# Wider small products and extra dense products on TensorE around the attentions and behind the experts of a four-layer transformer kernel

## What is computed

```python
o = jnp.stack(outs, axis=2) * alpha[..., None].astype(h.dtype)
return o.reshape(b, s, ATTN_WIDTH) @ w_o
...
for e in range(N_EXPERTS):
    out = out + gates[..., e:e + 1] * swiglu(h, w_gate[e], w_up[e], w_down[e])
```

## Time and profile before

| | |
|---|---|
| median of 3 runs | 2066.69 us (2065.45 to 2076.85) |
| the profiled execution's own time | 2066.5 us |
| its span, first to last instruction | 2064.3 us |
| mean granted TensorE clock over the span | 0.946 of full |
| TensorE busy | 1932.4 us (94%) |
| VectorE busy | 1639.3 us (79%) |
| ScalarE busy | 1138.9 us (55%) |
| DMA | 551.07 MB, mean 267 GB/s |

### The profile page before, as it was taken

How to read it: one execution, slowest core, us unless ns; L and a number is a source line. 1 busy time by engine, 2 the same in 40 slices (tenths; PEclk the granted TensorE clock), 3 DMA queues, 4 the chain that set the end, 5 groups by cost and what they waited for, 6 DMA issues and landing times.

```text
span 2064.3 us, 29232 instructions
## 1 busy us (share of the span) xinstructions
PE 1932.4 (94%) x9196; PEld 1602.1 (78%) x9196; DVE 1639.3 (79%) x2173; ACT 1138.9 (55%) x1616; POOL 36.1 (2%) x47
## 2 busy tenths in 40 slices
PE   2998999989899999999999999988899999789998
PEld 2987888867688888888888888866778888677886
DVE  6988886757898989998888989897686659677554
ACT  1434444443677777777777777654444444545443
POOL 2000000000000000000000000000000000000000
PEclk9999999977899999999999999987699999879999
DMA  8977996545699999999999999957368875735662
GB/s 290 340 248 268 346 360 199 148 157 176 201 358 335 366 340 368 330 366 335 344 355 340 361 337 363 339 173 218 111 223 265 270 243 145 255 123 175 218 217 73
DMA packets 368361, 551.07 MB, mean 267 GB/s; under 512 B 35715, under 2 KB 292998, under 8 KB 368230
## 3 DMA queue, kind: packets, MB, share of 16 engines
q1 hardware_dynamic: 365280, 547.81, 79.1%
q10 hardware_dynamic: 2118, 1.46, 0.2%
q0 software_dynamic: 832, 0.30, 0.1%
HBM read 548.38 MB, written 1.08 MB: 266 GB/s over the span
## 4 chain that ended last, share of the span: by engine, by line
PE 83%; DVE 10%; ACT 3%; issue 2%; DMA 2%; POOL 0%; DVEq 0%; ACTq 0%; SPq 0%; POOLq 0%
PE ps L399 24%; PE ps L401 23%; PE ps L400 23%; PE ps L875 3%; DVE units_low L394 2%; PE ps L864 2%; PE ps L1044 2%; PE ps L929 2%; DVE mod_acc L1544 1%; PE ps L726 1%; ACT prob L1237 1%; DVE x_tokens L1571 1%; PE ps L852 1%; DVE x_normed L1570 1%; ACT units_high L390 1%
## 5 line engine op out<-in xcount | busy, mean ns | idle before, releaser
L394 DVE TENSOR_TENSOR units_low<-raw_units,units_high 128x1024 fp32r<-128x1024 f32 (+2 forms) x840 | 982.9, 1218 | 116.7 <-ACT units_high L390 110.8
L390 ACT ACTIVATE units_high<-raw_units 128x1024 fp32r<-128x1024 f32 (+2 forms) x840 | 845.5, 1058 | 239.8 <-PE ps L401 224.8
L399 PE MATMUL ps<-units_high,hT_high 128*128 128x512 f32 (+2 forms) x1576 | 619.7, 393 | 4.5 <-DVE act L1640 2.9
L401 PE MATMUL ps<-units_high,hT_low 128*128 128x512 f32 (+2 forms) x1576 | 617.6, 392 | 0.0
L400 PE MATMUL ps<-units_low,hT_high 128*128 128x512 f32 (+2 forms) x1576 | 615.7, 391 | 0.0
L399 PEld LDWEIGHTS ps<-units_high,hT_high 128*128 128x128 f32 (+1 forms) x1576 | 296.8, 188 | 72.2 <-DVE act L1640 3.6
L400 PEld LDWEIGHTS ps<-units_low,hT_high 128*128 128x128 f32 (+1 forms) x1576 | 296.6, 188 | 64.3 <-issue 0.2
L401 PEld LDWEIGHTS ps<-units_high,hT_low 128*128 128x128 f32 (+1 forms) x1576 | 296.6, 188 | 63.9
L399 PE MATMUL ps<-units_high,aT_high 128*128 128x512 f32 x632 | 259.4, 410 | 1.2 <-DVE qkT L1781 0.6
L400 PE MATMUL ps<-units_low,aT_high 128*128 128x512 f32 x632 | 249.2, 394 | 0.0
L401 PE MATMUL ps<-units_high,aT_low 128*128 128x512 f32 x632 | 249.1, 394 | 0.0
(11 more groups left out here) (273 smaller groups left out, 1473.8 us busy)
## 6 DMA issues: line engine op xcount, KB each, us to landing
raw_units<-in_moe_w_gate SPq DMA_DIRECT2D x352, 256.0 KB, 4.5
raw_units<-in_moe_w_up SPq DMA_DIRECT2D x352, 256.0 KB, 5.6
raw_units<-in_moe_w_down SPq DMA_DIRECT2D x176, 512.0 KB, 5.9
mod_in<-in_mod_w SPq DMA_DIRECT2D x96, 512.0 KB, 6.1
mod_in<-in_w_mod SPq DMA_DIRECT2D x96, 512.0 KB, 5.2
raw_units<-in_w_gu SPq DMA_DIRECT2D x176, 256.0 KB, 3.3
raw_units<-in_w_down SPq DMA_DIRECT2D x44, 512.0 KB, 4.2
raw_units<-in_w_in SPq DMA_DIRECT2D x32, 512.0 KB, 7.0
```

What stands on the lines that cost most here:

```text
L390: eng.activation(whi[:rows, n % H, 0:width], raw[:rows, n % R, 0:width], ACT.Copy).then_inc(f.hi, 1)
L394: eng.tensor_tensor(low[:rows, n % R, 0:width], raw[:rows, n % R, 0:width], whi[:rows, n % H, 0:width].bitcast(F32), ALU.subtract).then_in ...
L399: pe.matmul(dst, ah, bh, start=start, stop=False, **kw)
L401: return pe.matmul(dst, al, bh, start=False, stop=stop, **kw)
```

## The change

It has three parts. (1) `sum_cols` takes all 128 columns of `ones` as its moving operand: each product writes 128 equal columns, and the next one overwrites all but the first. (2) In the PV products, a head whose next neighbour in the same PSUM bank comes later in the order takes that neighbour's 64 columns along, else one whose previous neighbour comes later takes those (`beside_later`); the 64 extra columns are overwritten by the neighbour's own product. (3) A new function `bridge(count, bank)` sends `count` fp32r products of 128 x 128 by 128 x 512 on `hT_high` to a PSUM bank whose content isn't used. It is called ahead of `normed_T` for s = 1, 3 and 4 (14, 12, 22 products), ahead of the attentions (5, 4, 4), at steps 1 and 2 of each attention (4 each), and ahead of `y_transposes` of the second and third attention (14 each). No wait, no DMA and no instruction of another engine is changed.

```diff
+BRIDGE = (0, 14, 0, 12, 22, 0, 0, 0)
+BRIDGE_IN, BRIDGE_PAIR, BRIDGE_OUT = (5, 4, 4), 4, (0, 14, 14)
...
-                last = pe.matmul(ps[:, 7, at + c:at + c + 1], cols_acc(m)[:, c * P:(c + 1) * P], ones[:, 0:1],
+                last = pe.matmul(ps[:, 7, at + c:at + c + P], cols_acc(m)[:, c * P:(c + 1) * P], ones,
                                  start=True, stop=True)
...
+        def bridge(count, bank):
+
+            for _ in range(count):
+                pe.matmul(ps[:, bank, :], hTh[:, 0, 0:P], hTh[:, 0:2, :].rearrange("p a b -> p (a b)"),
+                          start=True, stop=True)
+
         def normed_T(s):
 
+            bridge(BRIDGE[s], 6)
             if s:
                 pe.wait_ge(s_mga, 4 if s == 3 else s)
...
+        def beside_later(order, j):
+
+            later = [h for h in order[j + 1:] if h // 8 == order[j] // 8]
+            if order[j] + 1 in later:
+                return 0, 1
+            return (1, 0) if order[j] - 1 in later else (0, 0)
+
         def attention(a):
...
+            bridge(BRIDGE_IN[a], 0)
             for p in range(pairs + 2):
+                if 1 <= p <= 2:
+                    bridge(BRIDGE_PAIR, 0 if p == 1 else 3)
                 if p and p < pairs:
                     pe.wait_ge(s_max, i0 + 2 * p)
...
+                    left, right = beside_later(order, j)
                     for qt in range(T):
-                        dst = ps[:, 2 * qt + h // 8, (h % 8) * HD:(h % 8 + 1) * HD]
+                        dst = ps[:, 2 * qt + h // 8, (h % 8 - left) * HD:(h % 8 + 1 + right) * HD]
                         nk = key_tiles(second, qt)
                         for kt in range(nk):
+                            at = kt * width + v
                             last = pe.matmul(dst, probT[:, j % 2, qt * key_tiles(second, 0) + kt, :],
-                                             qkv[:, kt * width + v:kt * width + v + HD],
+                                             qkv[:, at - left * HD:at + (1 + right) * HD],
                                              start=kt == 0, stop=kt == nk - 1)
...
             chunks = W1 // KR if a == 0 else DC
+            bridge(BRIDGE_OUT[a], 6)
             for pair in range(chunks // 2):
```

## The result

The changed kernel takes **2044.1 us** (median of 4 runs, 2040.2 to 2046.1); the kernel before took 2069.6 beside it (2065.5 to 2076.9). The ratio is 0.987, with a 95% interval from 0.984 to 0.991: faster by more than the 0.5% that can be told. The two profiled spans, 2064.3 and 2042.5 us, differ by 21.8 us; 36 were forecast, and the range of 2015 to 2053 holds the result.

The account below looks back on a forecast made before the run. TensorE, busy 94% of the span, was taken to set the end, with 223 us at 1.2 GHz. Attentions 24.5, output's transposes 4 and norms 9.5, less 2, gave 36 us: 2066.5 - 36 = 2030.5 us, range 2015 to 2053.

Parts of the forecast that it names:

- rival 1: Attentions: the clock stays low despite wider PV, only the entry is helped; 13 to 14 us gained, 2053 us; chance 0.11.
- rival 2: Attentions and norms: transposes do not count for the clock, which falls in them; 21 us gained, 2045 us; chance 0.03.
- rival 4: Added dense products do not lift the clock, run at 0.43 us and overrun their gaps by 11 us; 2077 us; chance 0.04.
- Rival 3: Attentions and norms: VectorE or ScalarE gives back what TensorE gains; 2058 us, no change that can be told; chance 0.07.
- Cost of wider products: Foldings and PV: up to 128 moving columns pass beneath the load of the stationary columns; 0 us, at most 13 for PV.
- Cost of the dense products: At full speed each added group fits into a gap where TensorE waits for VectorE or ScalarE; 0 us, within 0.1.
- The attentions: Three attentions at full clock: 11 + 13.5 + 10 = 35 us gained; 70% taken, 24.5.
- The output's transposes: Transposes behind the three attentions at full clock: 1.9 + 1.7 + 1.7 = 5 us gained; 80% taken, 4.
- The norms: Norm transposes, folding and stretch ahead of the experts: 7.5 + 1 + 1.8 + 1 = 11 us gained; 85% taken, 9.5.
- The double folding: Folding of modulations 2 and 3: some 18 of its 64 records leave the slow stretch, 1.8 us gained.
- The routing: Slow TensorE stretch ahead of the experts, mostly small router products and waits: 1 us gained.
- the 2 for slow filling: Deduction of 2 us from the forecast gain for filling products that fall into a slow stretch.

Follow-up runs that it names:

- Folding on one column: The changed kernel with the folding of the modulation columns on one column again, all else kept: 2049.6 us, 0.989 of the kernel before.
- everything held: Changed kernel with first dense products ahead of the waits, 14 products in every pair, 7, 21, 21 ahead of the outputs, more in the routing: 2024.0 us.

## Why the prediction was right, and where its sizes were off

**The mechanism: shown.** In this kernel columns moved, not busy time, hold the clock. Three edits that change nothing but the width say so: 128 against 4 columns in the pairs' waits (0 against 24 us low in the attentions), 128 against 64 in PV (31 against 110 us low), and 128 against 1 in the foldings. The Trainium skill, "TensorE: Matmul & The Clock Gate", section "Part 1: The HAM clock gate (the "warmup" mystery)", speaks of how busy the engine has been; read as busy time, that does not fit here. The clock does not stay low (75 us, not some 200; rival 1), transposes count (rival 2), and the dense products of the change all run at full clock, most of them 0.23 us apart (rival 4; one overrun is in "Folding on one column"). Rival 3 falls for the attentions, but holds in part at the norms: there ScalarE and VectorE take over.

**Cost of wider products, set to 0: right.** 0.05 us a pair for PV; one folding of 32 records takes 3.73 us of 128 columns, against 3.69 of one column.

**Cost of the dense products, set to 0: wrong at one place.** "5 are 1.2 (2.73)" counted the gap ahead of the scores, but not on which side of the wait the call stands: in the code it is behind the last wait on the copied queries and keys, so the gap stays and the products come after it. Measured 1.3 + 1.1 + 1.1 = 3.5 us, returned when they were put ahead of it.

**The attentions, 35 if all holds and 24.5 forecast: near.** With everything held the three came down by 11.3, 13.4 and 9.5 = 34.2 us to the last PV, against 11 + 13.5 + 10. The change itself gained 7.5 + 9.5 + 5.3 = 22.3, or 65% where 70 was taken; that share was a guess, and its being close is partly luck, since the low stretches fall differently from one profile to the next. Another 2.4 are given back at once: once PV ends sooner, ScalarE's and VectorE's work on the last heads leads, and the output's transposes start 19.9 us sooner, not 22.3.

**The output's transposes, +4 forecast: wrong, -1.5.** "14 are 3.2 us ... in 5.06" left a wait of 2.5 us unfilled (the gap had also grown to 5.7), and the clock fell behind it, onto the transposes and the first products. The forecast also counted 1.9 us of the first attention's output, ahead of which the change sets no dense products (36.7 us before and after). With 7, 21 and 21 products it held; then this way is 1.2 + 1.0 + 1.0 = 3.2 us shorter than before, so the 5 for full holding was also too much.

**The norms, 9.5 forecast: 5.9.** The term was mis-sized: 1.5 a place, but 0.66 measured at five places. The chain shows why: 0.86 of the transposes and then 1.8 of ScalarE's and VectorE's copies now lead to the first product, so the remaining 1 us that TensorE saved is waiting; and no slow first products were left to gain (one of 0.43 in the earlier trace rows). Norm 4 gave 0 where 1 was taken. The double folding gave 1.8 as forecast. The routing gave 0.8 for 1, but it varies by more than that between profiles (18.8 to 23.4 us), so the agreement shows nothing.

**The sum**, between the two profiled spans: 19.9 - 1.5 + 5.9 - 3.5 = 20.8. The first 158 us came out 1.4 shorter (norm 1 begins at 158.1 here and between 158.1 and 162.4 in the other profiles), and the expert loop 0.4 longer: 21.8. Against the forecast of 36 (24.5 + 4 + 9.5 - 2), 4.6 went missing in the attentions and their ends, 5.5 at the outputs, 3.6 at the norms, and 3.5 on the chain ahead of the scores, of which the 2 for slow filling pays a part.

**The best version** holds all waits and reaches 2024.0 us, 20 below the change and 49 below the kernel before. With PV back at 64 columns it takes 2022.5, and the two can't be told apart.

Still open: why the clock falls in one pair and holds in the next like it; and whether the products added to the routing decide anything there, since it took 18.0 and 19.6 us with them and 18.8 to 23.4 without. Each kernel has one profile, so what is said of single stages rests on one execution each.

## What to carry to other kernels

Where TensorE runs at its lower clock though it is busy, look in a slow stretch at the columns per record, not at busy time, and widen records to the 128 columns that cost nothing here, or fill waits with such products. Put a filler ahead of the wait that it is to fill, and let it reach to the end of that wait: a call one line too late put it on the chain, and one 2.5 us too short lost the clock at 9 of 14 places just where the next work began. When TensorE's time halves, follow the chain again at each place, since behind a norm six of sixteen transposes were all that still counted.

## What the runs showed of the hardware

- Products of 4 and of 128 columns on fresh 128x128 weights take the same, 0.12 us a record at 2.4 GHz, and 0.22 at 1.2 GHz with 4 columns. What bounds such a record, presumably the loading of its weights, so follows the clock. The Trainium skill, "TensorE: Matmul & The Clock Gate", section "LDWEIGHTS (loading the stationary operand)", gives a load as its columns over 1.2, with no term for the clock; for 128 columns that is 107 ns, an estimate worked out from its formula. The record at full clock is near it, the one at half clock is not.
- In the first attention, TensorE busy for every one of 10.2 us was granted 1.2 GHz throughout, with products of 4 columns in the waits; with 128 columns in the same places the whole attention was granted 2.4 GHz.
- Fourteen float32 transposes a pair held the clock nearly as well as fourteen products of 128 columns did: 3.4 and 0 us low in the three attentions, against 24 with 4 columns.
